# The down projection's residual: products with alpha times the identity, or transposes of a stream scaled in place

## What is computed

```python
def _swiglu(h, w_in, w_out):
    gate, up = jnp.split(h @ w_in, 2, axis=-1)
    return (jax.nn.silu(gate) * up) @ w_out

DEEPNORM_ALPHA = (2.0 * DEPTH) ** 0.25          # 1.189
h = _layer_norm(DEEPNORM_ALPHA * h + _swiglu(h, ffn_w_in[l], ffn_w_out[l]), ln3_g[l], ln3_b[l])
```

## Time and profile before

| | |
|---|---|
| Median of 3 runs | 1162.82 us (1161.99 to 1163.18) |
| Span of the profiled execution, from its first to its last instruction | 1160.0 us |
| Instructions | 16855 |
| TensorE busy (products) | 1123.7 us, 97% |
| TensorE busy (weight loads, beside the products) | 901.7 us, 78% |
| VectorE / ScalarE / GpSimd busy | 535.9 / 435.7 / 500.6 us |
| Mean granted TensorE clock | 0.995 of 2.4 GHz |

### The profile page before, as it was taken

The page is one execution under the profiler, slowest core; times in us unless marked ns, Lnnn a source line. Parts: engine busy times, 40 slices in busy tenths (PEclk is TensorE's granted clock), DMA queues, the critical chain, the costliest instruction groups (busy, mean ns, idle before and its releaser), DMA issues.

```text
span 1160.0 us, 16855 instructions
## 1 busy us (share of the span) xinstructions
PE 1123.7 (97%) x6109; PEld 901.7 (78%) x6109; DVE 535.9 (46%) x1121; ACT 435.7 (38%) x766; POOL 500.6 (43%) x320
## 2 busy tenths in 40 slices
PE   6999999999999999999999999979999999999996
PEld 6888888887885666668887786758888888888885
DVE  7999941420247666756445716373322322310006
ACT  4342324311247666753334624146223223221211
POOL 5642442440234444555555740337444444434442
PEclk9999999999999999999999999999999999999999
DMA  6642432772121000013343430223333333323222
GB/s 193 93 108 56 123 91 56 253 188 46 37 74 37 1 1 2 2 62 103 101 132 124 135 90 19 73 73 110 92 107 91 92 107 91 93 75 105 91 95 87
DMA packets 158384, 101.68 MB, mean 88 GB/s; under 512 B 18344, under 2 KB 145968, under 8 KB 158192
## 3 DMA queue, kind: packets, MB, share of 16 engines
q1 hardware_dynamic: 153408, 94.48, 29.2%
q10 hardware_dynamic: 4912, 6.35, 1.7%
HBM read 93.59 MB, written 2.10 MB: 82 GB/s over the span
## 4 chain that ended last, share of the span: by engine, by line
PE 82%; DVE 10%; issue 4%; POOL 2%; ACT 1%; DMA 0%; DVEq 0%; POOLq 0%; ACTq 0%
PE bank L1402 77%; PE bank L1726 3%; POOL wlo L827 2%; DVE Pw L896 1%; DVE xc L896 1%; DVE cm L896 1%; DVE Sr L1210 1%; DVE bank L1296 1%; DVE hLo L896 0%; DVE bnst L915 0%; DVE sp_th L967 0%; DVE Ptmp L896 0%; DVE xmax L1341 0%; PE bank L1451 0%; PE bank L1535 0%
## 5 line engine op out<-in xcount | busy, mean ns | idle before, releaser
L827 POOL TENSOR_TENSOR wlo<-wraw,whi 128x1024 fp32r<-128x1024 f32 x160 | 392.9, 2457 | 513.7 <-ACT whi L503 513.7
L503 ACT ACTIVATE whi<-wraw 128x1024 fp32r<-128x1024 f32 x160 | 169.4, 1060 | 545.3 <-PE bank L1402 191.0
L1402 PE MATMUL bank<-hHi,whi 128*128 128x512 f32 x736 | 289.8, 394 | 8.6 <-ACT hHi L543 6.8
L1402 PE MATMUL bank<-hHi,wlo 128*128 128x512 f32 x736 | 287.6, 391 | 0.0
L1402 PE MATMUL bank<-hLo,whi 128*128 128x512 f32 x736 | 282.7, 389 | 0.0
L1402 PEld LDWEIGHTS bank<-hHi,whi 128*128 128x128 f32 x736 | 138.8, 189 | 40.1 <-ACT hHi L543 7.6
L1402 PEld LDWEIGHTS bank<-hHi,wlo 128*128 128x128 f32 x736 | 138.8, 189 | 29.4
L1402 PEld LDWEIGHTS bank<-hLo,whi 128*128 128x128 f32 x736 | 138.2, 188 | 28.0
L867 POOL TENSOR_SCALAR Sr<-Sr,winv,gates 128x512 f32<-128x512 f32 (+3 forms) x128 | 76.5, 607 | 78.6 <-DVE winv L1221 78.5
L896 DVE TENSOR_TENSOR sLo<-sF,sHi 128x512 f32 x22 | 50.0, 2275 | 98.1 <-ACT sHi L768 98.1
L688 ACT ACTIVATE Sr<-Sr,nmax 128x512 f32<-128x512 f32 (+3 forms) x128 | 71.7, 560 | 43.9 <-DVE nmax L1210 42.1
(11 more groups left out here) (315 smaller groups left out, 1725.9 us busy)
## 6 DMA issues: line engine op xcount, KB each, us to landing
wraw<-in_ffn_w_in SPq DMA_DIRECT2D x88, 256.0 KB, 3.1
wraw<-in_w_in SPq DMA_DIRECT2D x80, 256.0 KB, 3.3
wraw<-in_ffn_w_out SPq DMA_DIRECT2D x44, 256.0 KB, 2.8
wraw<-in_xattn_w_kv SPq DMA_DIRECT2D x32, 256.0 KB, 3.1
w<-in_cmp_w ACTq DMA_DIRECT2D x1, 4096.0 KB, 20.3
wraw<-in_nsa_w_out SPq DMA_DIRECT2D x16, 256.0 KB, 3.0
wraw<-in_w_out SPq DMA_DIRECT2D x16, 256.0 KB, 3.1
wraw<-in_xattn_w_q SPq DMA_DIRECT2D x16, 256.0 KB, 3.1
```

The source lines that it names most:

```text
L503: act.activation(hi_of(c)[:, :], wraw[c % 4][:, :], ACT.Copy).then_inc(w_hi_ready, 1)
L827: pool.tensor_tensor(wlo[c % 4][:, :], wraw[c % 4][:, :], hi_of(c)[:, :].bitcast(F32), ALU.subtract).then_inc(w_lo_ready, 1)
L1402: return pe.matmul(o, w, a, start=start, stop=stop)
```

## The change

VectorE no longer makes `alpha_w`. In its place, after the second normalization, it multiplies each of the eight pieces of `hF` by alpha in place, each as soon as POOL has made `hLo` from it. TensorE waits for all eight (`alpha_ready` at 8 in place of 1, and no wait for `hf_ready`). The 32 instructions keep their order, their banks, `hF` as the loaded operand and their start flags, but have `ident` as the moving operand and are marked as transposes.

```diff
-    alpha_w = at("alpha_w", [P, P], RC + 512)
@@
             normalize(2, lambda m: None)
-            dve.tensor_scalar(alpha_w[:, :], ident[:, :], ALPHA, None, ALU.mult).then_inc(alpha_ready, 1)
+            for m in range(KT):
+                dve.wait_ge(hlo_ready, 2 * KT + m + 1)
+                dve.tensor_scalar(hF[:, m, :], hF[:, m, :], ALPHA, None, ALU.mult).then_inc(alpha_ready, 1)
@@
-            pe.wait_ge(alpha_ready, 1)
-            pe.wait_ge(hf_ready, 2 * KT)
+            pe.wait_ge(alpha_ready, KT)
             for a in (2, 3, 0, 1):
                 if a == 0:
                     pe.wait_ge(sf_ready, KF + 2)
                 for half in range(2):
                     for m in range(4):
-                        mm(bank[2 * a + half][:, P * m:P * m + P], hF[:, 4 * half + m, P * a:P * a + P], alpha_w[:, :],
-                           m == 0, False)
+                        pe.matmul(bank[2 * a + half][:, P * m:P * m + P], hF[:, 4 * half + m, P * a:P * a + P],
+                                  ident[:, :], start=m == 0, stop=False, is_transpose=True)
             pe.wait_ge(slo_ready, KF)
```

## The result

The changed kernel takes 1158.76 us, the median of 8 runs (1158.39 to 1159.62), the kernel before beside it 1162.23 us (1161.89 to 1163.18): the ratio is 0.9963, with a 95% interval of 0.9947 to 0.9979. That is 3.5 us less. The profiled execution took 1158.39 us with a span of 1156.6 us.

The account below looks back on a forecast made before the run. TensorE, busy 97% of the span, was taken as the bound. Products of 7.06 us replaced by turns of 3.33 give 3.73 less, all else 0: 1162.82 - 3.73 = 1159.1 us, range 1158.3 to 1161.3.

Parts of the forecast that it names:

- the sum: Whole kernel: 7.06 - 3.33 = 3.73 us less, nothing for waits, weights and scalings; from 1162.82 to 1159.1 us.
- The turns: Block before the down projection: 32 transposes at 0.104 us, 3.33 us in place of 7.06; bounds 3.17 and 4.1.
- The bound: From 782.94 to 1151.18 us TensorE runs unbroken, so a microsecond saved in the block is one of the whole.
- Rival 2: At the block: the transpose flag brings nothing, a second pass is still made; 1162.8 us, chance 0.07.
- Rival 3: Turns idle the clock at the block: 1164.2 us, chance 0.04; only the products behind slow: 1160.9, chance 0.07.
- The reading of the first turns: Kernel start: 18 turns at 0.208 us, twice 0.104; only the first product behind slow, so turns counted as work.
- The rule of the Trainium skill: For transposes on TensorE the full clock "doesn't engage", as they do not count as busy in the same way.
- The wait on `sLo`: Before the down projection: last `sLo` ready 0.85 us before TensorE needs it, cost nothing; 0.8 us if its piece lasts 2.36.
- The scalings: VectorE after the second normalization: eight at 0.536 us, four pushing POOL 0.54 us each; cost nothing, bounds 0 and 0.9 us.
- The weights: Down projection: blocks wanted 3.7 us earlier, later ones loaded 16.3 us ahead of use against 7.2 needed; cost nothing.
- The spread of the span: Whole kernel: profiled span 1160.0 us to become 1156.3; 0.6 us was allowed for the runs' spread.

Follow-up runs that it names:

- the first comparison: The changed kernel, no further edit, measured beside the kernel before: 1158.76 us against 1162.23 us, ratio 0.9963.
- the second: The changed kernel measured again without an edit, on one chip with the kernel before: 1158.69 us against 1162.30 us, ratio 0.9966.
- the filled start: The changed kernel plus 56 idle turns in the second normalization's wait, 36 before the kernel's first turns and 10 between its second and third token tile: 1157.41 us.
- the filled kernel before: The kernel before plus 56 idle turns in TensorE's wait for the second normalization: 1161.74 us, ratio 0.9983.

## Why the prediction was right or wrong

The path, the mechanism and the direction held; what failed are sizes in the sum. Two of them enter the time that was forecast. The turns, at 32 x 0.104 = 3.33 us, measured 3.41. And the time from which the 3.73 us were taken was too high: the step says that the median stands 2.8 us above the span and that this part lies outside the instructions. In all executions on record the time is 1.75 to 1.94 us above the span; the other 1.0 us or so was that the profiled execution was faster than the median of three. That median, 1162.82 us, lies 0.6 us above the 1162.23 of eight. 1162.23 - 3.73 would have been 1158.5; the forecast of 1159.1 came within 0.3 us of the measured 1158.76 because the base, 0.6 us too high, made up for the gain, 0.3 us too large. That is luck. The 0.3 us of the gain (3.73 against 3.47 in the medians) are 0.08 from the turns; the rest is within what executions differ by, and the profiles have 0.2 of it ahead of the block (0.70 more at the lower clock, 0.49 less before).

- **The bound** was right: TensorE without a gap from the second normalization to the end, before and after, and 3.65 us less in the block are 3.5 to 3.6 us less in the median, with a difference of up to 1.2 us between executions from the clock behind the normalization.
- **The turns** were sized at 3.33 us and took 3.41, 0.107 each (0.1085 in the long run): a little above the row that I took, well inside the bounds. That is the main term of the sum, and 3.65 of its 3.73 us came. The median fell by 3.5 us on the first comparison and 3.6 on the second.
- **Rival 2** (a second pass in any case) fell by the 32 records, and the opposite edit, products with the identity, took all of the gain back.
- **Rival 3** (the clock) fell. The reading of the first turns was right in both halves: they were slow by the clock, as the filled start shows, and they counted as work. The rule of the Trainium skill that I weighed there (TensorE: Matmul & The Clock Gate, "Part 4: PE-mode transpose") does not hold for the float32 turns of this kernel: 128 turns in a row kept the clock at 1.00, and 56 of them kept it up in a wait in which it otherwise falls to 0.50.
- **The wait on `sLo`** came as worked out: 0.9 us of cover (0.85 forecast). What this step may lack is the second price of a wait. I had put 0.8 us on one; without the block 2.6 us of waiting cost 1.7 us more through the clock. Whether a wait of 0.8 us would cost any clock no run shows.
- **The scalings** were rightly put at nothing, but their working was off. I let each of four push POOL by 0.54 us, 2.2 us in all; the trace has 0.1 us over the `hLo` pieces, and the last is ready at 794.5 us, not between 795 and 797. POOL's pieces come every 1.4 us as without scalings, and it was mostly VectorE that waited: its scalings lasted from 0.41 to 2.61 us beside them. How the two share their turns in detail the trace does not show. I took 0.54 us from the scaling of `xtok`; in a row these took 0.33.
- **The weights** were rightly put at nothing, but the reason fails at the last block. I gave all later blocks three blocks, 16.3 us, between release and use. The last three blocks are read together, token tile by token tile. In the kernel before the last one's slot is free at 1031.22 + 18 x 5.44 = 1129.1 us, and it is wanted after the 19 whole blocks and 12 products, at 1137.3: 8.2 us, and loading and splitting took 7.3. POOL's last low part, before and after:

```profile
1134.00 2.39 POOL L827 TENSOR_TENSOR wlo<-wraw,whi 128x1024 fp32r<-128x1024 f32 x1 [3.06 <-ACT whi L503]
...
1130.62 2.39 POOL L826 TENSOR_TENSOR wlo<-wraw,whi 128x1024 fp32r<-128x1024 f32 x1 [3.30 <-ACT whi L502]
```

The last low part is ready at 1136.4 us in the one and 1133.0 in the other, 0.9 us ahead of its use in both, and the filled kernel before ran through this cover by 0.25 us. It did not matter here because release and use move together.

- **The spread of the span** was left out: the forecast span of 1156.3 us came out at 1156.6. The number of products at the lower clock behind the normalization differs between executions and cost 0.70 us between the two profiles, and the way to that place was 0.49 us shorter; it differs from trace to trace of all kernels (782.1 to 785.2 us).

## What to carry to other kernels

A float32 product with the identity, made only to turn or to carry data over, costs two passes here and a transpose one: 0.221 against 0.107 us for 128x128. Multiplying by a constant can go to an engine that has time, in place, if the spot between the last reader of the unscaled values and the turn is free. And ask of every wait on the bounding engine what it does to the clock behind it: 2.6 us of waiting cost 1.7 us more in slow products, and filling a wait of 6.8 us with idle work, turns or products, gained 1.5 to 1.8 us on top of the change, almost half as much again as the change itself. In the kernel before the same filling gained only 0.7 us, which its interval does not tell from nothing; why is open.

## What was not expected of the hardware

- Transposes hold TensorE's clock at its full level as well as products do (1.00 through 14 us of turns, and behind them).
- The clock can fall at short waits too, but need not: behind 2.6 us without work products were 0.43 us apart, the lower level (1.2 GHz), and behind 1.9 us at the start the granted clock was 0.57 over 18 turns, while a wait of 2.3 us shortly before, in the same run, left the turns behind it at 0.113 us each.
- The record of the granted clock can't be trusted at the start of an execution: it reads 1.00 over the kernel's first 14 turns, which took 0.215 us each, and the same 14 took 0.113 us once idle turns had been run ahead.
- VectorE's scaling of 128x512 in float32, SBUF to SBUF, costs 0.33 us when many follow each other. Eight of them, each behind one of POOL's `hLo` pieces, delayed POOL by 0.1 us over eight pieces; 24 more without pause stretched one POOL piece from 2.4 to 5.4 us, though VectorE worked on without pause beside it.
